# Attention scores from high and low parts, one buffer for the queries, query evacuations held back by a slot

## The chip, the cores and the metric

One core of a Trainium2 chip runs the whole program. The time is device microseconds of one execution. Three executions of the kernel before gave 1408.58, 1412.33 and 1412.37 us; the median is 1412.33. The engines are named as the profile names them: PE is TensorE, DVE VectorE, ACT ScalarE, POOL GpSimd, SP SyncE.

## What is computed

A block of a model: mLSTM mixer, cross attention to a memory, gated feed-forward, each with a norm ahead and a residual. The change touches the cross attention alone (sequence 1024, memory 256, 4 heads of 256, all float32):

```python
def cross_attn(xn, memn, w_q, w_kv, w_o):
    q = (xn @ w_q).reshape(Bsz, S, X_HEADS, X_DH)
    k, v = jnp.split(memn @ w_kv, 2, axis=-1)
    ...
    s = jnp.einsum('bshd,bmhd->bhsm', q, k).astype(F32) * (X_DH ** -0.5)
    p = jax.nn.softmax(s, axis=-1).astype(v.dtype)
    o = jnp.einsum('bhsm,bmhd->bshd', p, v).reshape(Bsz, S, D)
    return o @ w_o
```

## The kernel before

Every engine has its own program, written out by hand, and the programs meet only at semaphores. The order is set by strips of weights, 256 columns or rows wide. For the attention the list is mk 0 to 3 (keys), the last wo, mv 0 to 3 (values), q 0, then q 1, xo 0, q 2, xo 1, q 3, xo 2, and xo 3. A q strip makes the queries of one head in 4 groups (`r` 0 to 3; `r % 2` is the half of the head's 256 features, `r // 2` the half of the 1024 tokens), each of 24 matmuls of 512 columns into one bank of PSUM. An xo strip has 16 groups of 6 matmuls and adds one head's part of the output projection to the residual `xT`. Banks 0 to 3 of PSUM are taken in turn; `FREED` says which engine's count frees a bank, and `wait_bank` waits for it before the bank's next group.

Nearly every product on TensorE is made from two fp32r parts of each operand (`product`, lines 1861 to 1869): high by high, high by low, low by high. The high part is a copy on ScalarE into an fp32r tile, the low part is the rest, subtracted on VectorE. The scores are the exception: line 2069 multiplies `QH` (queries) by `KM` (keys) as plain fp32. A plain fp32 matmul has two records in the trace.

Work besides the groups hangs on `PARTS`, which gives each engine a list of parts ahead of group `r` of a strip. Head h's attention is `attn(h, p)`. Parts 0 to 3 stand ahead of groups 0 to 3 of strip q h+1, parts 4 and 5 ahead of groups 0 and 3 of strip xo h; for the last head parts 0 to 3 are at groups 4, 7, 9 and 12 of xo 2, and 4 and 5 at groups 1 and 4 of xo 3. For a tile of 256 tokens (p from 0 to 3) the work is: TensorE scores (L2069) into bank 4 or 5; VectorE maximum (L1472, L1473); ScalarE exponentials into `ptok`, which is `acc` (L977); in part p+1, VectorE reciprocal and normalising (L1464, L1466), TensorE four transposes (L2079), ScalarE high part `PAH` (L987), VectorE low part `PAL` (L1478). Parts 3 and 5 multiply by the values and split the result into `YH` and `YL` (L998, L1485), which the xo strip reads.

Query groups are copied out of PSUM by ScalarE (L1054), right behind each group, into two places used in turn: `VQ` for even heads and `SG` for odd ones. Keys lie in `KM`, values in `VM` (both in full fp32), and the values are split in strip q 0 by `vsplit` (L1003 and L1491). Beside all this the weights of the next strip are split: high on ScalarE behind the parts of slot 0 (L874), low on VectorE in slots 1 and 2 (L1574). VectorE adds the residual of each xo group (L1500). Each engine carries out its program in the order written.

Of the kernel before, what the change touches and what calls it, by code (L numbers as in the profile page):

```python
# [6 lines left out]
ALU = mybir.AluOpType  # L7
# [3 lines left out]
P = 128  # L11
# [5 lines left out]
def build_block(nc, x, mem, norm_mix, norm_x, norm_ffn, norm_mem, norm_final, a_w_in, a_conv_w, a_gate_b,  # L17
# [26 lines left out]
    for h in range(1, H):  # L44
# [5 lines left out]
    assert NF % 2 == 0  # L50
    NGROUPS = {"qk": 4, "v": 4, "o": 4, "wo": 16, "mk": 1, "mv": 1, "q": 4, "xo": 16,
               "gate": 4, "up": 4, "last": 24}
    BY_ACT = {"v", "o", "mk", "mv", "q", "gate"}
    FIRST, FREED, took = {}, [], {"act": 0, "dve": 0, "up": 0}
    GROUPS = [(n, r) for n, (kind, _) in enumerate(STRIPS) for r in range(NGROUPS[kind])]
    at = GROUPS.index((NF, 0))
# [10 lines left out]
    NB = 4  # L67
# [19 lines left out]
    def part(kind, h, r, what):  # L87
        PARTS.setdefault((AT[kind, h], r), []).append(what)
# [45 lines left out]
    for i in range(4):  # L134
        part("xo", H - 1, 12 + i, ("pieces", 4, (2 * i, 2 * i + 1)))
    for t in range(2):
        part("q", 0, 1 + t, ("vsplit", t, None))
    for h in range(1, H):
        for p in range(4):
            part("q", h, p, ("attn", h - 1, p))  # L140
# [23 lines left out]
    with ctx:  # L164
# [18 lines left out]
        def sem(name):  # L183
            return ctx.enter_context(nc.semaphore(name))
# [84 lines left out]
        ML = XL[:, 0:2, :].rearrange("p k s -> p (k s)").rearrange("p (k m) -> p k m", k=KT)  # L269
        KM = QK[:, 0].rearrange("p a s -> p (a s)").rearrange("p (k m) -> p k m", k=KT)  # L270
        VM = VQ[:, 0].rearrange("p (a d) -> p a d", a=MT)
        QH = [VQ[:, 1].rearrange("p (a s) -> p a s", a=2), SG[:, :, :]]
        ptok = acc[:, :, :]
        halves = lambda t: t.rearrange("p (a s) -> p a s", a=2)
        sqb = [None, halves(SG[:, 1, :]), acc[:, :, :]]
# [18 lines left out]
        S3L = sb_at("S3L", [P, 4, HALF], vv_at, F32R)  # L294
        PAH = sb_at("PAH", [P, MT, S], qk_at + 8192, F32R)
        PAL = sb_at("PAL", [P, MT, S], scan_at, F32R)
        VMH = sb_at("VMH", [P, MT, D], late_at, F32R)
        VML = sb_at("VML", [P, MT, D], vv_at, F32R)
        four = lambda t: t[:, :, :].rearrange("p a (b s) -> p (a b) s", b=2)
# [105 lines left out]
        s_mu = sem("s_mu")  # L405
        s_st = sem("s_st")
        s_wt = sem("s_wt")
        s_mask = sem("s_mask")
        s_wi = sem("s_wi")
        s_ks = sem("s_ks")  # L410
        s_pt = sem("s_pt")
# [16 lines left out]
        s_pt2 = sem("s_pt2")  # L428
        s_pa = sem("s_pa")
        s_pah = sem("s_pah")  # L430
        s_vmh = sem("s_vmh")
        s_vml = sem("s_vml")
        s_pv = sem("s_pv")
        s_sqn = sem("s_sqn")
        s_ssq = sem("s_ssq")
# [297 lines left out]
        def _(pool):  # L733
# [73 lines left out]
                        gp.tensor_tensor(lo, full, hi.bitcast(F32), ALU.subtract).then_inc(s_xlp, 1)  # L807

            todo = {"scan": scan, "memnorm": memnorm, "sumsq": sumsq, "pieces": pieces}
            for what in ("gates", "memturn", "spread", "attn", "vsplit"):  # L810
                todo[what] = lambda a, b: None

            sumsq(0, 0)
# [53 lines left out]
        def _(act):  # L867
# [132 lines left out]
            def vsplit(t, b):  # L1000

                act.wait_ge(s_fa, FREED[FIRST[AT["mv", H - 1]]][1])
                sc.activation(VMH[:, t, :], VM[:, t, :], ACT.Copy).then_inc(s_vmh, 1)  # L1003

            todo = {"gates": gates, "scan": scan, "memnorm": memnorm, "memturn": memturn,
                    "pieces": pieces, "attn": attn, "vsplit": vsplit}
            for what in ("sumsq", "spread"):
                todo[what] = lambda a, b: None

            def evac(n, r):  # L1010
                kind, h = STRIPS[n]
                g = FIRST[n] + r
                bank = PS[:, g % NB, :]
                if kind == "qk":

                    c = 4 * h + r
                    act.wait_ge(s_conv, c + 1)
                    if r == 0 and h >= 2:
                        act.wait_ge(s_b, TT * (h - 1))
                    at = (r // 2) * HALF  # L1020
                    sc.activation(QK[:, h % 2, r % 2, at:at + HALF], acc[:, r % 2, :], ACT.Tanh, scale=0.5).then_inc(s_ex1, 1)
                    return
                if kind not in BY_ACT:
                    return
                act.wait_ge(s_mm, g + 1)
                if kind == "v":
                    if r == 0 and h >= 2:
                        act.wait_ge(s_b, TT * (h - 1))
                    sc.activation(VV[:, h % 2, 2 * r:2 * r + 2, 0:DV], bank.rearrange("p (t d) -> p t d", t=2),
                                  ACT.Copy).then_inc(s_fa, 1)  # L1030
                elif kind == "o":
                    if r == 0 and h == 0:
                        act.wait_ge(s_gd, 5)
                    if r == 0 and h >= 1:
                        act.wait_ge(s_yf, TT * h)
                    sc.activation(SG[:, r % 2, (r // 2) * HALF:(r // 2 + 1) * HALF], bank,
                                  ACT.Tanh, scale=0.5).then_inc(s_fa, 1)
                elif kind == "mk":
                    if h == 0:
                        act.wait_ge(s_turn, TT + MT)  # L1040
                        act.wait_ge(s_xs, MT)
                    sc.activation(KM[:, 2 * h:2 * h + 2, :], bank.rearrange("p (t d) -> p t d", t=2),
                                  ACT.Copy).then_inc(s_fa, 1)
                elif kind == "mv":
                    sc.activation(VM[:, :, h * SW:(h + 1) * SW], bank.rearrange("p (t d) -> p t d", t=2),
                                  ACT.Copy).then_inc(s_fa, 1)
                elif kind == "q":
                    if r == 0 and h == 0:
                        act.wait_ge(s_b, TT * H)
                    if r == 0 and h == 1:  # L1050
                        act.wait_ge(s_xl, LO[3, LATE[1]][1])
                    if r == 0 and h >= 2:
                        act.wait_ge(s_sc, 4 * (h - 1))
                    sc.activation(QH[h % 2][:, r % 2, (r // 2) * HALF:(r // 2 + 1) * HALF], bank,  # L1054
                                  ACT.Copy).then_inc(s_fa, 1)

            def square_x(t):
# [22 lines left out]
            for n in range(NF):  # L1080
                kind, h = STRIPS[n]
                for r in range(NGROUPS[kind]):
                    run_parts(n, r, todo)
                    if r == 0:
                        split_hi(n + 1)
                        if held:
                            evac(*held.pop())
                    if NGROUPS[kind] == 1:
                        run_parts(n, "mid", todo)
                    if kind == "o" and h >= 1:  # L1090

                        if r == 3:
                            for q in range(4):
                                evac(n, q)
                    elif (kind, h) == ("wo", H - 1) or (kind, h) == ("xo", H - 1) and r < KT + 3:
                        square(n, r)
                    elif kind == "mv":
                        held.append((n, r))
                    else:
                        evac(n, r)  # L1100
                run_parts(n, "end", todo)
# [158 lines left out]
        def _(dve):  # L1260
# [67 lines left out]
            def scan(h, p):  # L1328
                if p < TT:
                    e = h * TT + p  # L1330
                    dve.wait_ge(s_wt, e + 1)
                    v.tensor_tensor(wT[:, e % 2, :], wT[:, e % 2, :], causal[:, :], ALU.min).then_inc(s_mask, 1)
                    dve.wait_ge(s_st, e + 1)
                    dve.wait_ge(s_mask, e + 1)
                    if e >= 2:
                        dve.wait_ge(s_b, e - 1)
                    v.scalar_tensor_tensor(out=wT[:, e % 2, :], in0=X1[:, 2 * P:3 * P], scalar=QSCALE, in1=wT[:, e % 2, :], op0=ALU.mult,
# [149 lines left out]

            def vsplit(t, b):

                dve.wait_ge(s_vmh, t + 1)  # L1490
                v.tensor_tensor(VML[:, t, :], VM[:, t, :], VMH[:, t, :].bitcast(F32), ALU.subtract).then_inc(s_vml, 1)  # L1491

            todo = {"gates": gates, "scan": scan, "memnorm": memnorm, "memturn": memturn, "vsplit": vsplit,
                    "sumsq": sumsq, "spread": lambda a, b: None, "pieces": pieces, "attn": attn}

            def add_residual(g, r):

# [4 lines left out]
            def evac(n, r):  # L1502
# [26 lines left out]
                elif kind == "v" and r == 0:  # L1529
                    finish_qk(h, 3)  # L1530
                elif kind == "o" and r == 3:
                    for q in range(4):
                        finish_o(n, q)
                elif kind not in BY_ACT:
                    add_residual(g, r)

# [25 lines left out]
            for n in range(NF):  # L1562
                kind, h = STRIPS[n]
                with_squares = kind in ("wo", "xo") and h == H - 1
                which = 1 if kind == "wo" else 2
                for r in range(NGROUPS[kind]):
                    run_parts(n, r, todo)
                    if kind == "mk":
                        run_parts(n, "mid", todo)
                    if NGROUPS[kind] == 1 or r in (1, 2):  # L1570
# [274 lines left out]
        def _(pe):  # L1845
# [209 lines left out]
            def attn(h, p):  # L2055
                if p < 4:
# [5 lines left out]
                    if p == 0 and h:  # L2062
                        pe.wait_ge(s_yl, H * TT + 4 * h)
                    if p == 0:
                        pe.wait_ge(s_fa, FREED[FIRST[AT["q", h]] + 3][1])
                    for j in range(2):
                        at = slice((2 * p + j) * P, (2 * p + j + 1) * P)
                        for kk in range(2):
                            last = mm(PS[:, NB + e % 2, j * M:(j + 1) * M], QH[h % 2][:, kk, at], KM[:, 2 * h + kk, :],  # L2069
                                      start=(kk == 0), stop=(kk == 1))  # L2070
                    last.then_inc(s_sc, 1)
                if 1 <= p <= 4:
                    e = 4 * h + p - 1
# [8 lines left out]
                if p in (3, 5):  # L2082
                    half = p // 2 - 1
                    pe.wait_ge(s_pa, 4 * h + 2 * half + 2)
                    for dt in range(2):
# [5 lines left out]
                        if p == 3 and dt == 1:  # L2091
                            pe.wait_ge(s_ex, 2 * (4 * h + 3))
                        if c == 0:
                            pe.wait_ge(s_vml, MT)
                        v_at = slice(h * DV + dt * P, h * DV + (dt + 1) * P)
                        p_at = slice(half * HALF, (half + 1) * HALF)
                        product((X3, X0)[dt], [((VMH[:, m, v_at], VML[:, m, v_at]), (PAH[:, m, p_at], PAL[:, m, p_at]))
                                               for m in range(MT)]).then_inc(s_pv, 1)

            todo = {"gates": gates, "scan": scan, "memnorm": lambda a, b: None, "memturn": memturn, "sumsq": sumsq,  # L2100
                    "spread": spread, "pieces": lambda a, b: None, "attn": attn, "vsplit": lambda a, b: None}

            def turn_x(t):

# [184 lines left out]
```

## Time and profile before

| | |
|---|---|
| median of 3 runs | 1412.33 us |
| profiled execution | 1410.57 us |
| its span, first to last instruction | 1408.8 us |
| mean granted clock of TensorE | 0.995 |
| PE busy | 1374.4 us, 98%, 6833 matmul records |
| PEld (weight loads) busy | 1162.9 us, 83% |
| DVE busy | 943.4 us, 67% |
| ACT busy | 492.4 us, 35% |
| POOL busy | 209.0 us, 15% |
| line 2069 in the chain that ended last | 1.9% of the span |

The query and output strips run from about 507 to 745 us. A row of a timeline gives the start in us, the duration in us, the engine, the line, the operation and its tiles (out<-in), shapes, a count, and in brackets the idle time of the engine before it and what ended that. Matmuls are pipelined: a 512-column one has a duration of 0.39 us and the next starts 0.23 us later, so the pace is read from starts. Equal tiles and shapes in a row are merged, as in "x8". The idle time of an engine that nobody waits for costs nothing.

### The profile page before, as it was taken

To read this page: it belongs to the slowest core of one execution; us is meant where nothing else is said; L and a number is where in the kernel's file an instruction comes from. 1 tells how busy PE (TensorE), PEld (TensorE's weight loads), DVE (VectorE), ACT (ScalarE), POOL (GpSimd) and SP (SyncE) were. 2 spreads that over 40 slices of the span, in tenths; PEclk is the share of its full clock that TensorE was granted. 3 is DMA by queue.
4 is the path that set the end of the run, shared out by engine and by line. 5 is a ranking of instruction groups with operands and counts; after the bars stand their busy time and mean duration, and the time that the engine had idled before them with its cause. 6 is when DMAs were issued, how large, how long until landed. Compare 5 with 4: busy or idle time off the path is not lost.

```text
span 1408.8 us, 18109 instructions
## 1 busy us (share of the span) xinstructions
PE 1374.4 (98%) x6833; PEld 1162.9 (83%) x6833; DVE 943.4 (67%) x1660; ACT 492.4 (35%) x868; POOL 209.0 (15%) x228
## 2 busy tenths in 40 slices
PE   7999999999998999999999999999999998999997
PEld 6988888889888878888877888888888887888887
DVE  5838458458377863554577976677787778877775
ACT  6323213313335453222334533343444434222222
POOL 5001201202303000000005000000000004444441
PEclk9999999999999999999999999999999999999999
DMA  5111201200313220010132132244444449799603
GB/s 181 41 50 31 60 31 31 60 30 31 105 61 107 74 88 32 30 60 7 54 120 105 46 113 98 75 165 159 140 142 164 145 168 366 263 305 316 237 30 120
DMA packets 109255, 156.44 MB, mean 111 GB/s; under 512 B 6448, under 2 KB 67952, under 8 KB 109168
## 3 DMA queue, kind: packets, MB, share of 16 engines
q1 hardware_dynamic: 109168, 155.28, 32.5%
q8 instruction: 55, 0.90, 0.3%
q14 instruction: 32, 0.26, 0.1%
HBM read 112.79 MB, written 42.47 MB: 110 GB/s over the span
## 4 chain that ended last, share of the span: by engine, by line
PE 64%; DVE 3%; issue 1%; ACT 0%; POOLq 0%; POOL 0%; ACTq 0%; DVEq 0%
PE PS L2185 9%; PE PS L2183 9%; PE PS L2184 9%; PE PS L1866 7%; PE PS L1867 6%; PE PS L1868 6%; PE PS L2213 4%; PE PS L2215 4%; PE PS L2214 4%; PE PS L2069 2%; DVE SG L1416 1%; PE PS L2079 0%; DVE xT L1500 0%; PE PS L2247 0%; DVE QK L1449 0%
## 5 line engine op out<-in xcount | busy, mean ns | idle before, releaser
L1866 PE MATMUL PS<-XH,WH 128*128 128x512 f32 (+1 forms) x448 | 174.8, 390 | 3.4 <-issue 3.3
L1868 PE MATMUL PS<-XH,WL 128*128 128x512 f32 (+1 forms) x448 | 168.5, 376 | 0.0
L1867 PE MATMUL PS<-XL,WH 128*128 128x512 f32 (+1 forms) x448 | 168.5, 376 | 0.0
L1500 DVE TENSOR_TENSOR xT<-PS,xT 128x512 f32<-128x512 f32 x128 | 87.6, 688 | 46.9 <-PE PS L1868 46.4
L1708 DVE TENSOR_TENSOR xT<-PS,xT 128x512 f32<-128x512 f32 x120 | 80.8, 688 | 43.2 <-PE PS L2215 42.9
L1866 PE MATMUL PS<-YH,WH 128*128 128x512 f32 x256 | 101.7, 397 | 0.7 <-issue 0.7
L1866 PEld LDWEIGHTS PS<-XH,WH 128*128 128x128 f32 x448 | 84.7, 189 | 19.5 <-issue 4.4
L1868 PE MATMUL PS<-YH,WL 128*128 128x512 f32 x256 | 99.8, 390 | 0.0
L1867 PE MATMUL PS<-YL,WH 128*128 128x512 f32 x256 | 99.7, 390 | 0.0
L1868 PEld LDWEIGHTS PS<-XH,WL 128*128 128x128 f32 x448 | 84.7, 189 | 15.8
L1867 PEld LDWEIGHTS PS<-XL,WH 128*128 128x128 f32 x448 | 84.7, 189 | 14.6
L1866 PE MATMUL PS<-WH,XH 128*128 128x256 f32 x320 | 92.6, 289 | 2.0 <-issue 2.0
L1868 PE MATMUL PS<-WH,XL 128*128 128x256 f32 x320 | 90.5, 283 | 0.0
L1867 PE MATMUL PS<-WL,XH 128*128 128x256 f32 x320 | 90.5, 283 | 0.0
L841 POOL TENSOR_TENSOR W2A<-raw,W2A 128x512 fp32r<-128x512 f32 x20 | 27.6, 1379 | 386.6 <-ACT W2A L1170 386.6
L1648 DVE TENSOR_TENSOR U<-PS,U 128x512 f32<-128x512 f32 x50 | 33.6, 688 | 55.7 <-PE PS L2185 55.7
L1574 DVE TENSOR_TENSOR WL<-raw,WH 128x1024 fp32r<-128x1024 f32 x54 | 65.8, 1227 | 5.0 <-ACT WH L874 5.0
L1866 PEld LDWEIGHTS PS<-WH,XH 128*128 128x128 f32 x320 | 61.2, 191 | 2.9 <-issue 2.4
L2183 PE MATMUL PS<-XH,WA 128*128 128x512 f32 x160 | 62.2, 389 | 0.0
L2185 PE MATMUL PS<-XH,WA 128*128 128x512 f32 x160 | 62.2, 389 | 0.0
L2183 PE MATMUL PS<-XH,WB 128*128 128x512 f32 x160 | 62.2, 389 | 0.0
L2185 PE MATMUL PS<-XH,WB 128*128 128x512 f32 x160 | 62.2, 389 | 0.0
(386 smaller groups left out, 3467.8 us busy)
## 6 DMA issues: line engine op xcount, KB each, us to landing
forms_hi<-HS SPq DMA_DIRECT2D x56, 256.0 KB, 2.4
raw<-in_f_w_up_dram SPq DMA_DIRECT2D x11, 1024.0 KB, 5.8
rawE<-in_f_w_gate_dram SPq DMA_DIRECT2D x10, 1024.0 KB, 5.7
raw<-in_f_w_down_dram SPq DMA_DIRECT2D x40, 256.0 KB, 3.8
raw<-in_a_w_in_dram SPq DMA_DIRECT2D x8, 1024.0 KB, 5.2
forms_lo<-U SPq DMA_DIRECT2D x32, 256.0 KB, 2.6
XH<-forms_hi SPq DMA_DIRECT2D x16, 512.0 KB, 6.4
XL<-forms_lo SPq DMA_DIRECT2D x12, 512.0 KB, 7.0
```

The lines of the kernel that those rows point to most:

```text
L1500: v.tensor_tensor(xt, PS[:, g % NB, :], xt, ALU.add).then_inc(s_fd, 1)
L1574: last = v.tensor_tensor(WL[:, (n + 1) % 2, at], raw_of(n + 1)[:, at], WH[:, (n + 1) % 2, at].bitcast(F32), ALU.subtract)
L1708: v.tensor_tensor(x, bank_of(g, which), x, ALU.add).then_inc(s_ee, 1)
L1866: mm(dst, wh, xh, start=(k == 0), stop=False)
L1867: mm(dst, wh, xl, start=False, stop=False)
L1868: last = mm(dst, wl, xh, start=False, stop=(k == len(tiles) - 1))
L2183: mm(bank, w[:, i, 0, at], xh[:, kk, :], start=start, stop=False, skip_group_check=True)
L2184: mm(bank, w[:, i, 0, at], xl[:, kk, :], start=False, stop=False, skip_group_check=True)
L2185: last = mm(bank, w[:, i, 1, at], xh[:, kk, :], start=False, stop=stop, skip_group_check=True)
L2213: mm(bank, w[:, i, 0, at], xh[:, u, :], start=start, stop=False, skip_group_check=True)
L2214: mm(bank, w[:, i, 0, at], xl[:, u, :], start=False, stop=False, skip_group_check=True)
L2215: last = mm(bank, w[:, i, 1, at], xh[:, u, :], start=False, stop=stop, skip_group_check=True)
```

## The change

The keys are split into `KMH` (heads 0 to 2 in one tile, head 3 in another) and `KML`, which lies where `KM` lies; this is the new part `ksplit`, two steps on ScalarE and VectorE in groups 1 and 2 of q 0, and `vsplit` moves one group later. The queries get one high tile `QHH` and one low tile `QHL` for all heads. ScalarE writes the high part, and VectorE subtracts it from the bank in `query_lo`; the bank is freed by VectorE now. Line 2069 becomes a `product` of high and low parts: twelve fp32r matmuls of 256 columns for a tile of 256 tokens where there were four plain ones. The evacuation of query group r is done in slot r+1, behind that slot's parts; that of group 3 at the head of the next strip, ahead of its parts, on ScalarE and on VectorE. A new wait on ScalarE keeps `QHH` until the scores of the head before have read it. In the scan of the mixer a wait for a semaphore of its own (`s_mask`) becomes the common chain of VectorE (`link`).

```diff
@@ ordering
-    BY_ACT = {"v", "o", "mk", "mv", "q", "gate"}
+    BY_ACT = {"v", "o", "mk", "mv", "gate"}
...
     for t in range(2):
-        part("q", 0, 1 + t, ("vsplit", t, None))
+        part("q", 0, 1 + t, ("ksplit", t, None))
+        part("q", 0, 2 + t, ("vsplit", t, None))
@@ tiles
-        QH = [VQ[:, 1].rearrange("p (a s) -> p a s", a=2), SG[:, :, :]]
+        KMH = [sb_at("KMH", [P, 6, M], late_at + 8192, F32R), sb_at("KMT", [P, 2, M], scan_at + 8192, F32R)]
+        KML = sb_at("KML", [P, 2 * H, M], qk_at, F32R)
+        QHH = sb_at("QHH", [P, 2, S], vv_at + 8192, F32R)
+        QHL = sb_at("QHL", [P, 2, S], place["SG"], F32R)
@@ ScalarE
+            def ksplit(t, b):
+
+                act.wait_ge(s_fa, FREED[FIRST[AT["mk", H - 1]]][1])
+                act.wait_ge(s_yl, H * TT)
+                sc.activation(KMH[t][:, :, :], KM[:, 6 * t:6 + 2 * t, :], ACT.Copy).then_inc(s_kvh, 1)
...
+                if kind == "q":
+                    act.wait_ge(s_mm, g + 1)
+                    if r == 0 and h == 0:
+                        act.wait_ge(s_b, TT * H)
+                    if r % 2 == 0 and h >= 1:
+                        act.wait_ge(s_sc, 4 * (h - 1) + 2 + r)
+                    sc.activation(QHH[:, r % 2, (r // 2) * HALF:(r // 2 + 1) * HALF], bank, ACT.Copy).then_inc(s_qh, 1)
                     return
...
                 for r in range(NGROUPS[kind]):
+                    if r == 0 and held and STRIPS[held[0][0]][0] == "q":
+                        evac(*held.pop())
                     run_parts(n, r, todo)
                     if r == 0:
                         split_hi(n + 1)
...
+                    elif kind == "q":
+                        if r:
+                            evac(*held.pop())
                         held.append((n, r))
@@ VectorE
-                    v.tensor_tensor(wT[:, e % 2, :], wT[:, e % 2, :], causal[:, :], ALU.min).then_inc(s_mask, 1)
+                    link(v.tensor_tensor(wT[:, e % 2, :], wT[:, e % 2, :], causal[:, :], ALU.min))
                     dve.wait_ge(s_st, e + 1)
-                    dve.wait_ge(s_mask, e + 1)
...
+            def ksplit(t, b):
+
+                dve.wait_ge(s_kvh, 2 * t + 1)
+                at = slice(6 * t, 6 + 2 * t)
+                v.tensor_tensor(KML[:, at, :], KM[:, at, :], KMH[t][:, :, :].bitcast(F32), ALU.subtract).then_inc(s_kvl, 1)
...
+            def query_lo(n, r):
+
+                hi, lo = (t[:, r % 2, (r // 2) * HALF:(r // 2 + 1) * HALF] for t in (QHH, QHL))
+                dve.wait_ge(s_qh, 4 * STRIPS[n][1] + r + 1)
+                v.tensor_tensor(lo, PS[:, GI[n, r] % NB, :], hi.bitcast(F32), ALU.subtract).then_inc(s_fd, 1)
...
+                elif kind == "q":
+                    split_late.append((n, r))
...
                 for r in range(NGROUPS[kind]):
+                    if r == 0 and split_late:
+                        query_lo(*split_late.pop())
                     run_parts(n, r, todo)
+                    if split_late:
+                        query_lo(*split_late.pop())
@@ TensorE, attn
                     if p == 0:
-                        pe.wait_ge(s_fa, FREED[FIRST[AT["q", h]] + 3][1])
+                        pe.wait_ge(s_fd, FREED[FIRST[AT["q", h]] + 3][1])
+                        pe.wait_ge(s_kvl, 3)
                     for j in range(2):
                         at = slice((2 * p + j) * P, (2 * p + j + 1) * P)
-                        for kk in range(2):
-                            last = mm(PS[:, NB + e % 2, j * M:(j + 1) * M], QH[h % 2][:, kk, at], KM[:, 2 * h + kk, :],
-                                      start=(kk == 0), stop=(kk == 1))
+                        keys = lambda k: (KMH[k // 6][:, k % 6, :], KML[:, k, :])
+                        last = product(PS[:, NB + e % 2, j * M:(j + 1) * M],
+                                       [((QHH[:, kk, at], QHL[:, kk, at]), keys(2 * h + kk)) for kk in range(2)])
```

## Rows read from the trace of the kernel before

**Rows 1.** The page, busy time of each engine over the span.

```profile
PE 1374.4 (98%) x6833; PEld 1162.9 (83%) x6833; DVE 943.4 (67%) x1660; ACT 492.4 (35%) x868; POOL 209.0 (15%) x228
```

**Rows 2.** Busy us by stretch: PE, PEld, DVE, ACT, POOL, clock, DMA.

```profile
530.00:562.00 32.00, 31.77 (x147) 26.68 (x148) 11.93 (x27) 10.33 (x26) 0.00 (x0) 1.00 0.10 34
562.00:588.00 26.00, 26.00 (x118) 21.50 (x117) 14.62 (x20) 4.09 (x5) 0.00 (x0) 1.00 0.13 41
```

**Rows 3.** Timeline of PE, scores in two slots and their neighbours.

```profile
537.52 1.89 PE L2069 MATMUL PS<-QK,VQ 128*128 128x256 f32 x8
539.25 0.60 PE L2079 MATMUL PS<-ident,acc 128*128 128x128 f32 x4
...
587.45 0.39 PE L1866 MATMUL PS<-YH,WH 128*128 128x512 f32 x1
...
588.13 1.89 PE L2069 MATMUL PS<-QK,SG 128*128 128x256 f32 x8
...
590.55 0.39 PE L1866 MATMUL PS<-XH,WH 128*128 128x512 f32 x1
```

**Rows 4.** Timeline of PE: fp32r products of 256 columns; entry to 512 columns.

```profile
485.08 0.28 PE L1866 MATMUL PS<-WH,XH 128*128 128x256 f32 x1
485.20 0.28 PE L1867 MATMUL PS<-WL,XH 128*128 128x256 f32 x1
...
75.38 0.47 PE L1866 MATMUL PS<-XH,WH 128*128 128x512 f32 x1
75.69 0.40 PE L1867 MATMUL PS<-XL,WH 128*128 128x512 f32 x1
```

**Rows 5.** Timelines of ACT and PE at the start of q 1.

```profile
529.49 0.60 ACT L1054 ACTIVATE VQ<-PS 128x512 f32<-128x512 f32 x1 [4.84 <-PE PS L1868]
530.23 1.97 PE L2069 MATMUL PS<-QK,VQ 128*128 128x256 f32 x8 [0.78 <-ACT VQ L1054]
```

**Rows 6.** Timelines of DVE, PE and ACT around the start of xo 0.

```profile
559.35 0.62 DVE L1466 TENSOR_SCALAR acc<-acc,small 128x256 f32<-128x256 f32 x2
...
563.16 0.60 PE L2079 MATMUL PS<-ident,acc 128*128 128x128 f32 x4
...
563.36 0.60 ACT L1054 ACTIVATE SG<-PS 128x512 f32<-128x512 f32 x1 [4.85 <-PE PS L1868]
563.86 0.59 ACT L987 ACTIVATE PAH<-PS 128x512 fp32r<-128x512 f32 x1
...
564.48 0.69 DVE L1478 TENSOR_TENSOR PAL<-PS,PAH 128x512 fp32r<-128x512 f32 x1 [4.52 <-ACT PAH L987]
```

**Rows 7.** Timelines of DVE and PE at group 1 of xo 3.

```profile
717.18 0.69 DVE L1500 TENSOR_TENSOR xT<-PS,xT 128x512 f32<-128x512 f32 x1 [0.67 <-PE PS L1868]
...
718.64 0.66 PE L2079 MATMUL PS<-ident,acc 128*128 128x128 f32 x4 [1.50 <-DVE acc L1466]
```

**Rows 8.** Timeline of DVE in q 1; then line 1491 (duration ns min/median/max).

```profile
543.85 0.62 DVE L1466 TENSOR_SCALAR acc<-acc,small 128x256 f32<-128x256 f32 x2
...
L1491 DVE TENSOR_TENSOR VML<-VQ,VMH x2: 1218/1222/1227, 519.7 to 521.9; 128x1024 fp32r<-128x1024 f32 x2
```

**Rows 9.** Timeline of PE behind two gaps; stretches as in rows 2, with clock.

```profile
507.12 0.47 PE L1866 MATMUL PS<-XH,WH 128*128 128x512 f32 x1 [2.06 <-issue]
...
757.04 1.05 PE L2036 MATMUL PS<-ones,SG 128*128 128x1 f32 x8 [1.90 <-DVE SG L1416]
...
759.02 0.63 PE L1867 MATMUL PS<-XL,WH 128*128 128x512 f32 x1
759.45 0.63 PE L1868 MATMUL PS<-XH,WL 128*128 128x512 f32 x1
...
506.00:508.00 2.00, 0.88 (x4) 0.78 (x5) 2.00 (x3) 0.29 (x1) 0.00 (x0) 1.00 0.00 0
...
759.00:760.00 1.00, 1.00 (x4) 0.79 (x3) 0.00 (x0) 0.00 (x0) 0.68 (x1) 0.50 1.08 350
...
762.00:763.00 1.00, 1.00 (x5) 0.85 (x4) 0.00 (x0) 0.00 (x0) 0.00 (x0) 0.85 0.00 0
```

More of the change, by code:

```diff
@@ L407, in build_block @@
         s_wt = sem("s_wt")
-        s_mask = sem("s_mask")
         s_wi = sem("s_wi")
@@ L430, in build_block @@
         s_pah = sem("s_pah")
-        s_vmh = sem("s_vmh")
-        s_vml = sem("s_vml")
+        s_kvh = sem("s_kvh")
+        s_kvl = sem("s_kvl")
+        s_qh = sem("s_qh")
         s_pv = sem("s_pv")
@@ L809, in _ @@
             todo = {"scan": scan, "memnorm": memnorm, "sumsq": sumsq, "pieces": pieces}
-            for what in ("gates", "memturn", "spread", "attn", "vsplit"):
+            for what in ("gates", "memturn", "spread", "attn", "vsplit", "ksplit"):
                 todo[what] = lambda a, b: None
@@ L1002, in vsplit @@
                 act.wait_ge(s_fa, FREED[FIRST[AT["mv", H - 1]]][1])
-                sc.activation(VMH[:, t, :], VM[:, t, :], ACT.Copy).then_inc(s_vmh, 1)
+                sc.activation(VMH[:, t, :], VM[:, t, :], ACT.Copy).then_inc(s_kvh, 1)
+            def ksplit(t, b):
+                act.wait_ge(s_fa, FREED[FIRST[AT["mk", H - 1]]][1])
+                act.wait_ge(s_yl, H * TT)
+                sc.activation(KMH[t][:, :, :], KM[:, 6 * t:6 + 2 * t, :], ACT.Copy).then_inc(s_kvh, 1)
             todo = {"gates": gates, "scan": scan, "memnorm": memnorm, "memturn": memturn,
-                    "pieces": pieces, "attn": attn, "vsplit": vsplit}
+                    "pieces": pieces, "attn": attn, "vsplit": vsplit, "ksplit": ksplit}
             for what in ("sumsq", "spread"):
@@ L1021, in evac @@
                     sc.activation(QK[:, h % 2, r % 2, at:at + HALF], acc[:, r % 2, :], ACT.Tanh, scale=0.5).then_inc(s_ex1, 1)
+                    return
+                if kind == "q":
[5 more added lines that the diff above has]
+                    sc.activation(QHH[:, r % 2, (r // 2) * HALF:(r // 2 + 1) * HALF], bank, ACT.Copy).then_inc(s_qh, 1)
                     return
@@ L1046, in evac @@
                                   ACT.Copy).then_inc(s_fa, 1)
[L1047 to L1055, printed above, removed]
             def square_x(t):
@@ L1097, in _ @@
                     elif kind == "mv":
+                        held.append((n, r))
+                    elif kind == "q":
+                        if r:
+                            evac(*held.pop())
                         held.append((n, r))
@@ L1488, in vsplit @@
             def vsplit(t, b):
-                dve.wait_ge(s_vmh, t + 1)
-                v.tensor_tensor(VML[:, t, :], VM[:, t, :], VMH[:, t, :].bitcast(F32), ALU.subtract).then_inc(s_vml, 1)
-            todo = {"gates": gates, "scan": scan, "memnorm": memnorm, "memturn": memturn, "vsplit": vsplit,
-                    "sumsq": sumsq, "spread": lambda a, b: None, "pieces": pieces, "attn": attn}
+                dve.wait_ge(s_kvh, 2 * t + 2)
+                v.tensor_tensor(VML[:, t, :], VM[:, t, :], VMH[:, t, :].bitcast(F32), ALU.subtract).then_inc(s_kvl, 1)
+            def ksplit(t, b):
+                dve.wait_ge(s_kvh, 2 * t + 1)
+                at = slice(6 * t, 6 + 2 * t)
+                v.tensor_tensor(KML[:, at, :], KM[:, at, :], KMH[t][:, :, :].bitcast(F32), ALU.subtract).then_inc(s_kvl, 1)
+            todo = {"gates": gates, "scan": scan, "memnorm": memnorm, "memturn": memturn, "vsplit": vsplit, "ksplit": ksplit,
+                    "sumsq": sumsq, "spread": lambda a, b: None, "pieces": pieces, "attn": attn}
+            split_late = []
+            def query_lo(n, r):
+                hi, lo = (t[:, r % 2, (r // 2) * HALF:(r // 2 + 1) * HALF] for t in (QHH, QHL))
+                dve.wait_ge(s_qh, 4 * STRIPS[n][1] + r + 1)
+                v.tensor_tensor(lo, PS[:, GI[n, r] % NB, :], hi.bitcast(F32), ALU.subtract).then_inc(s_fd, 1)
             def add_residual(g, r):
@@ L2093, in attn @@
                         if c == 0:
-                            pe.wait_ge(s_vml, MT)
+                            pe.wait_ge(s_kvl, 2 * MT)
                         v_at = slice(h * DV + dt * P, h * DV + (dt + 1) * P)
@@ L2100, in _ @@
             todo = {"gates": gates, "scan": scan, "memnorm": lambda a, b: None, "memturn": memturn, "sumsq": sumsq,
-                    "spread": spread, "pieces": lambda a, b: None, "attn": attn, "vsplit": lambda a, b: None}
+                    "spread": spread, "pieces": lambda a, b: None, "attn": attn, "vsplit": lambda a, b: None, "ksplit": lambda a, b: None}
             def turn_x(t):
```

## Prediction

> **What bounds the kernel now.** I read the page's engine line first: TensorE is busy for 98% of the span [rows 1]. An average over stages does not say who is waited for in the attention, so the second view is the table of stretches. In the query strips and the output strips between them TensorE has no gap: 31.77 of 32 us, then 26.00 of 26, at a granted clock of 1.00, while VectorE works 11.93 and 14.62 us there and ScalarE 10.33 and 4.09 [rows 2]; the two stretches stand for five (530 to 678 us), which repeat them. So a microsecond taken from TensorE there is gained whole, and a microsecond for which TensorE waits is lost whole. Spare time of VectorE is cover only for work that TensorE doesn't wait for. The third view is the timeline of the places where the change puts something between TensorE and the operand that it needs next.
>
> I call the time in which TensorE makes one group of a strip a slot. "q1 slot 3" is the fourth group of ("q", 1).
>
> **The change part by part.**
>
> *Scores.* Sixteen times, four plain fp32 products of 256 columns (two records each) become twelve fp32r products. In a slot in which transposes follow, the scores run from 537.52 to 539.25, 1.73 us [rows 3]. The replacement has the form of the memory keys' products, 128x256 with a load of weights each, which start 0.12 us apart [rows 4]: 12 x 0.12 = 1.44 us, a gain of 0.29 in 12 places. In the 4 places where a group follows at once, the scores take from 588.13 to the second L1866 at 590.55, less the usual step 588.13 - 587.45 = 0.68, so 1.74 us [rows 3]; afterwards 1.44 and an entry to the next group like 75.38 to 75.69 (0.31 where 0.23 is the pace, and 0.03 before it) [rows 4], about 1.55: a gain of 0.19. Sum 12 x 0.29 + 4 x 0.19 = 4.2 us, all on TensorE's path. Bounds: 3.0 (0.19 everywhere) and 4.6 (0.29 everywhere).
>
> The Trainium skill (FP8 and Floating Point Precision, section on TensorE precision) gives true fp32 four passes, and TensorE: Matmul & The Clock Gate (Back-to-back issue gap) N/2.4 + 2.5 ns each; an estimate from these would be 64 x 109 ns = 7.0 us, and + 0.4 in place of + 3.2 in the sum below. The memory keys' rows are slower than that, 0.12 against 0.109, and they decide. The same page (Part 3, The mechanism) says that a weight load overlaps a running matmul only on another row group; with the loads in series the gain would be gone, and the sum 4.2 us higher. The pace of 0.12 us with one load each [rows 4] speaks against it here.
>
> *Splitting keys.* ScalarE gets two copies (1536 and 512 columns) and VectorE two subtractions in q0. The nearest VectorE row is the split of the values, 1.22 us for 1024 columns [rows 8], so about 1.8 and 0.65 us. VectorE starts at about 519.6 as before and then has 2.45 (keys) + 2.45 (values) + 2.4 (weights of q1) + three low parts at 0.65: done near 529, and the high part of q0's last group comes only at 530.1. Hidden, with 1 us to spare. The weights of q1 are ready near 527, the load for xo0 starts 2.5 us later than before, and both are wanted after 531.
>
> *Start of q1.* Before, TensorE waited for ScalarE's copy of q0's last group (start 529.49, scores at 530.23) [rows 5]. Now VectorE's low part stands behind it: 529.49 + 0.62 (from a ScalarE copy to the VectorE operation behind it, 563.86 to 564.48 [rows 6]) + 0.69 + 0.04 = 530.84. Cost 0.6 us; bounds 0.5 and 1.0.
>
> *Held evacuations inside the query strips.* The evacuation of group r is now behind the attention part of slot r+1 on both engines, and its bank is wanted four groups later. VectorE's extra 0.65 us per slot lies between the low part of the probabilities and the next normalising, which ends near 544.5 [rows 8] where the transposes that need it start about 546.9 (one slot of 7.6 us behind 539.25 [rows 3]): 2.4 us of slack, less 0.65 and less what the shorter scores take (0.3), leaves 1.4. Cost nothing; if the cover were gone, each us of overshoot would count in about eight slots. The new wait on the scores of the head before (one place for queries) is already met, since TensorE makes those scores at the head of the slot. The mask wait of the scan goes to an equivalent wait of VectorE on itself: nothing. SyncE and GpSimd get no instruction.
>
> *The last group of q1, q2 and q3.* This is the step that decides. In the first slot of xo0, xo1 and xo2 TensorE starts with four transposes of the normalised probabilities. Before, VectorE normalised them long ahead (559.35), and TensorE went through at 563.16 with no gap; ScalarE copied the last query group beside it (563.36) [rows 6]. After, VectorE has `query_lo` of that last group at the head of this slot, ahead of reciprocal and normalising. VectorE takes its work in order, so the normalising waits for the end of the matmuls, ScalarE's copy and the subtraction, and TensorE for all of it. The same kind of wait stands already in xo3: from the start of a 0.69 us operation through reciprocal and normalising to the transposes, 717.18 to 718.64, 1.46 us, with TensorE idle 1.50 [rows 7]. With the copy ahead: 563.36 + 0.62 + 1.46 = 565.44 instead of 563.16, so 2.28 us. Three times: 6.8 us. Bounds: 4.9 (3 x 1.64, as if the copy were free) and 7.5 (a quarter us of entry each). Everything behind moves along with TensorE, so nothing downstream gives it back.
>
> *The clock.* Rows of this trace show both ends for such a gap. After an idle 2.06 us the clock stayed at 1.00 (2.4 GHz); after an idle 1.90 and eight one-column products it fell to 0.50 (1.2 GHz) at 759.0 and came back near 762.3 [rows 9]. The new gap, 2.28 us and 0.36 of transposes, lies between these two (2.1 and 2.8 us without a dense matmul). So I take even odds for each, one or two of three. Price: matmuls start 0.43 apart instead of 0.23 for 3.3 us [rows 9], eight of them, 1.6 us for each fall; bounds none and 4.8 for all three.
>
> **Sum** on the profiled execution's own time, 1410.6 us (span 1408.8 and 1.8 around it): - 4.2 + 0.6 + 6.8 = + 3.2 before the clock; with one fall + 4.8, with two + 6.4. The middle is + 5.6, 1416.2 us. The median of the runs shown is 1.8 above the profiled execution, and they spread over 3.8; a change within 0.3%, 4.2 us, is about what a measurement of this kernel can't tell from none.
>
> **Rivals.**
> (a) The clock is held in all three gaps: + 3.2, 1413.8 us, which is no measurable change. For it: the 2.06 us gap that cost nothing [rows 9]. This ends on the other side; the point from which it decides is whether a gap of this length lets the clock fall.
> (b) All three gaps let it fall: + 8.0, 1418.6. For it: the fall at 759.0.
> (c) The gap in the xo strips doesn't come, because the normalising is finished before the low part: - 4.2 + 0.6 = - 3.6, 1407.0. The change would then do what a reader of TensorE's column alone expects. Against it: the order of VectorE's program, and the 1.50 us of xo3 [rows 7].
> (d) VectorE falls behind in q0 or inside the slots: up to 2 us more at q1 and in slots with a weight split, 1418 or so. Against it: 11.93 of 32 us busy [rows 2].
>
> **How the numbers follow.** The forecast (one or two falls) 0.50; (a) 0.29; (b) 0.11; (c) 0.05; (d) 0.05. Its own range is 1414 to 1418.5. One fall (+4.8) is just over the bound, so of the forecast's half I give 0.42 to slower, 0.07 to no change and 0.01 to faster (a pace of the products under 0.12); of (a), with the size of the stall uncertain, 0.06 and 0.23; (b) and (d) are slower but for 0.01; (c) is split, 0.03 to no change and 0.02 to faster. Slower 0.63, same 0.34, faster 0.03. The range takes in (a) less the bounds of its terms (1.9 on the stalls, 0.4 on the scores), (b), and the distance of the runs' median: 1411.5 to 1420.5.
>
> **What would show each step.** The scores' twelve products in 1.44 us, where 1.73 stood. TensorE idle about 2.3 us, three times, before L2079's transposes, released by VectorE's normalising, with `query_lo` right before the reciprocal. About 1.4 us idle before the first scores. In the table of stretches, 3 to 4 us of granted clock near 0.5 behind one or two of these gaps. No idle time inside the query strips. I am wrong if the transposes at the head of xo0 start without a gap, if the products start over 0.14 us apart, or if VectorE's normalising inside a query strip ends after the transposes could start.

## The result, and the profile after

The changed kernel takes 1416.67 us (median of 8 runs, 1414.65 to 1419.93) against 1410.88 us (8 runs, 1408.58 to 1412.56) before: + 5.8 us, ratio 1.0038 with a 95% interval of 1.0027 to 1.0049, which is + 3.8 to + 6.9 us. The forecast was + 5.6. The profiled execution of after took 1415.1 us (span 1413.4).

The page's engine line answers to [rows 1]. TensorE is busy 2.2 us less, in a span that is 4.5 us longer; columns as there.

```profile
PE 1372.2 (97%) x6897; PEld 1163.4 (82%) x6897; DVE 955.9 (68%) x1678; ACT 493.8 (35%) x870; POOL 208.8 (15%) x228
```

The timeline of PE in after, for the scores with transposes behind them (540.25) and with a group behind them (592.29), answers to [rows 3]:

```profile
538.81 0.28 PE L1900 MATMUL PS<-KMH,QHH 128*128 128x256 f32 x1
538.93 0.28 PE L1901 MATMUL PS<-KML,QHH 128*128 128x256 f32 x1
...
540.25 0.60 PE L2114 MATMUL PS<-ident,acc 128*128 128x128 f32 x4
...
590.85 0.28 PE L1900 MATMUL PS<-KMH,QHH 128*128 128x256 f32 x1
...
592.29 0.40 PE L1900 MATMUL PS<-XH,WH 128*128 128x512 f32 x1
592.98 0.40 PE L1900 MATMUL PS<-XH,WH 128*128 128x512 f32 x1
```

Twelve products take 538.81 to 540.25, 1.44 us, where 1.73 stood; the next group is entered at its normal step (592.29 to 592.98, 0.69). Now the start of q 1, ACT, DVE and PE in after, which answers to [rows 5]:

```profile
530.43 0.60 ACT L1039 ACTIVATE QHH<-PS 128x512 fp32r<-128x512 f32 x1 [4.84 <-PE PS L1902]
531.06 0.69 DVE L1522 TENSOR_TENSOR QHL<-PS,QHH 128x512 fp32r<-128x512 f32 x1 [3.13 <-ACT QHH L1039]
531.85 0.36 PE L1900 MATMUL PS<-KMH,QHH 128*128 128x256 f32 x1 [1.46 <-issue]
```

TensorE is idle for 1.46 us instead of 0.78. The profile puts it down to "issue", but the three rows stand in a row: copy, subtraction, first product 0.10 us behind it. VectorE had been idle for 3.13 us, so the split of the keys was out of the way. The rows that decide are those at the head of xo 0, in the same order; they answer to [rows 6]:

```profile
563.33 0.39 PE L1902 MATMUL PS<-XH,WL 128*128 128x512 f32 x1
...
563.75 0.60 ACT L1039 ACTIVATE QHH<-PS 128x512 fp32r<-128x512 f32 x1 [4.35 <-PE PS L1902]
...
564.38 0.69 DVE L1522 TENSOR_TENSOR QHL<-PS,QHH 128x512 fp32r<-128x512 f32 x1 [4.15 <-ACT QHH L1039]
564.99 0.15 DVE L1478 RECIPROCAL small<-small 128x2 f32<-128x2 f32 x1
565.18 0.62 DVE L1480 TENSOR_SCALAR acc<-acc,small 128x256 f32<-128x256 f32 x2
...
565.85 0.66 PE L2114 MATMUL PS<-ident,acc 128*128 128x128 f32 x4 [2.13 <-DVE acc L1480]
```

The last matmul of q 1 starts at 563.33, so with the pace of 0.23 the transposes were due at 563.56; they start at 565.85, 2.29 us late. VectorE, idle for 4.15 us ahead of this, could have normalised long before, but the low part of the last query group stood in front of it. xo 1 and xo 2 show the same:

```profile
624.82 0.66 PE L2114 MATMUL PS<-ident,acc 128*128 128x128 f32 x4 [2.14 <-DVE acc L1480]
683.79 0.66 PE L2114 MATMUL PS<-ident,acc 128*128 128x128 f32 x4 [2.14 <-DVE acc L1480]
```

The clock, stretches as in [rows 9], in after:

```profile
563.00:566.00 3.00, 0.86 (x5) 0.40 (x4) 1.38 (x4) 0.60 (x1) 0.00 (x0) 1.00 0.00 0
566.00:568.00 2.00, 2.00 (x12) 1.70 (x12) 0.76 (x2) 1.46 (x2) 0.00 (x0) 1.00 0.00 0
...
684.00:686.00 2.00, 2.00 (x9) 1.60 (x8) 0.69 (x1) 1.51 (x2) 0.00 (x0) 0.60 0.00 0
686.00:688.00 2.00, 2.00 (x7) 1.57 (x6) 1.01 (x2) 0.89 (x1) 0.00 (x0) 0.55 0.00 0
```

Behind the gap of xo 0 the clock stayed at 1.00; behind that of xo 2, of the same length, it fell to 0.50 for 3.4 us (684.4 to 687.8). One fall of three in this execution.

**The books of the stage.** From q 0's last matmul to xo 3's last one it is 529.07 to 743.87 before, 214.8 us, and 530.00 to 750.05 after, 220.1: + 5.3 us. Three gaps of 2.29 are 6.9, the start of q 1 0.7, one fall of the clock 1.6; together 9.2, so the shorter scores are left with 3.9. Line by line they give 16 x 0.29 = 4.6; the rest goes into entries behind the gaps (0.41 us from the transposes to the next group at 565.85, where it is 0.35 at 540.25) and small waits in xo 2. The 1.6 for a fall can be read from rows: from the transposes at the head of xo 2 to the next scores it is 10.76 us in after (683.79 to 694.55), and 9.17 in gap_short below (678.02 to 687.19), where the clock held, so 1.59.

### The profile page after: what moved, and what is told of

It reads as the page before. It is cut to its first block, busy times and chain, and to the rows that moved or that the text cites. A ratio compares the mean times of both kernels' runs of the same rounds, so it can differ in the third digit from the quotient of the medians.

```text
span 1413.4 us, 18265 instructions
## 1 busy us (share of the span) xinstructions
PE 1372.2 (97%) x6897; PEld 1163.4 (82%) x6897; DVE 955.9 (68%) x1678; ACT 493.8 (35%) x870; POOL 208.8 (15%) x228
## 4 chain that ended last, share of the span: by engine, by line
PE 88%; DVE 7%; issue 2%; DMA 1%; ACT 1%; SPq 1%; POOL 0%; POOLq 0%; DVEq 0%; ACTq 0%
PE PS L1900 14%; PE PS L1901 14%; PE PS L1902 14%; PE PS L2218 8%; PE PS L2220 8%; PE PS L2219 8%; PE PS L2248 4%; PE PS L2250 4%; PE PS L2249 4%; PE PS L2042 1%; PE PS L2046 1%; PE PS L2044 1%; DVE SG L1430 1%; PE PS L1963 1%; DVE xT L1528 1%
```

## Experiments

Times are medians, each with the ratio to the kernel before on the same chip; "before" is 1411.47 us (16 runs) for the first four kernels and 1409.80 us (15 runs) for the others. These are two chips: the kernel before is 1.7 us apart on them, and 0.2 when both are brought to one clock (how, stands under norm_first_early). A difference between kernels of the two groups is therefore given at one clock as well. The theory **order** says: VectorE's program order costs 2.29 us at each of three places. Its rivals are **load** (VectorE has too much to do, wherever it stands), **products** (the new products or their weight loads cost more than they show), and for the clock **count** (a gap costs only its own length), against **clock** (a gap can also let the clock fall) and **phase** (where the gap lies in time has a say in that).

**after_again** is the changed kernel once more.

> The changed kernel as it is, as the reference for its neighbours on this chip. Every theory: 5 to 6 us over the kernel before. Theory order (VectorE's low part of the last query group stands ahead of the normalising): three gaps of TensorE of 2.1 to 2.2 us idle at the heads of xo 0, 1 and 2. Theory phase (the clock falls behind a gap or not by where the gap lies in time, not by its length alone): the gaps are as long as in the first profile, but the clock may fall behind other ones of them.

Measured 1416.81 us (1.0040, 1.0027 to 1.0054). The gaps are 2.14 us idle again. The mean clock is 0.992 in the profile, and this time there are falls behind xo 2's gap, as in the first profile, and behind an older one at 760 us, where the first one had none. So at 760 us the same gap of the same program had a fall in one execution and none in the other; at the three new gaps the pattern stayed.

**norm_first** moves one operation of VectorE, three times.

```diff
-                    if r == 0 and split_late:
+                    if r == 0 and split_late and kind == "q":
                         query_lo(*split_late.pop())
                     run_parts(n, r, todo)
```

> One line: at the head of the xo strips VectorE does the attention part (reciprocal, normalising) first and query_lo after it; at the head of q 1 the order stays. Theory order: the three gaps vanish (3 x 2.29 = 6.9 us) and with them the clock falls behind them (0 to 4.8): 7 to 9 us below after_again, 1.5 to 3 us below the kernel before, since the shorter scores (16 x 0.3) less the longer wait at q 1 (0.7) are left. Rival load (VectorE is too full with the new splits, wherever they stand): the gaps stay or move into the slots, under 3 us gained. Rival products (the new products and their weight loads cost what the profile hides): still above the kernel before.

Measured 1407.75 us (0.9974, 0.9964 to 0.9984): 9.1 us below after_again and 3.7 below the kernel before. VectorE and PE of norm_first at the same place:

```profile
558.17 0.68 DVE L1522 TENSOR_TENSOR QHL<-PS,QHH 128x512 fp32r<-128x512 f32 x1
558.76 0.15 DVE L1478 RECIPROCAL small<-small 128x2 f32<-128x2 f32 x1
558.96 0.62 DVE L1480 TENSOR_SCALAR acc<-acc,small 128x256 f32<-128x256 f32 x2
...
562.17 0.60 PE L2114 MATMUL PS<-ident,acc 128*128 128x128 f32 x4
...
564.10 0.68 DVE L1522 TENSOR_TENSOR QHL<-PS,QHH 128x512 fp32r<-128x512 f32 x1
```

The normalising is done 2.6 us ahead of the transposes, which have no idle time, and the low part of the last group (564.10) stands behind the attention part. The work is the same, so load falls, and with it products: without the gaps the kernel is faster than the one before.

**norm_first_early** also lets TensorE start a head's scores once the groups of their tokens are there.

```diff
                     if p == 0:
-                        pe.wait_ge(s_fd, FREED[FIRST[AT["q", h]] + 3][1])
+                        pe.wait_ge(s_fd, FREED[FIRST[AT["q", h]] + 1][1])
                         pe.wait_ge(s_kvl, 3)
+                    if p == 2:
+                        pe.wait_ge(s_fd, FREED[FIRST[AT["q", h]] + 3][1])
```

> norm_first, and TensorE waits ahead of the first scores of a head only for the query groups 0 and 1, which hold the tokens of the first two tiles, and for groups 2 and 3 ahead of the third tile. Theory order: the idle time ahead of q 1's scores (1.46 us) goes, so 1.5 us below norm_first and about 4 us below the kernel before. Rival: the wait only moves, because groups 0 and 1 have their low parts late in q 0 (VectorE is busy with keys and values there); then under 0.5 us below norm_first.

Measured 1407.41 us (0.9967, 0.9954 to 0.9980). The idle time at q 1 is gone from the profile, as expected: in the waits of PE (us in total, times, longest) "issue" stands at 7.5 in 6 times in norm_first and here at

```profile
PE PS L1900 <- issue: 6.0, 5, 2.1
```

The medians differ by only 0.3 us, though, which is what the rival (the wait only moves) expected. The medians of this pair alone don't show the 1.5 us: the mean clock of the runs was 0.9930 here and 0.9948 in norm_first. Over all 91 runs of these kernels the time goes up by 0.93 us for each 0.001 of mean clock (one slope fitted within the kernels), and brought to one clock (0.994) the means of the pair are 1408.3 and 1406.6 us, 1.7 apart. The profiles say the same without a fit: from q 0's last matmul to xo 3's last one it is 211.3 us in norm_first and 209.6 here, with the clock at 1.00 throughout in both, so the wait did not move.

**before_stalled** puts the suspected wait alone into the kernel before.

```diff
                 for r in range(NGROUPS[kind]):
+                    if kind == "xo" and r == 0 and h < H - 1:
+                        dve.wait_ge(s_fa, FREED[FIRST[AT["q", h + 1]] + 3][1])
+                        v.tensor_tensor(T[:, 0].rearrange("p a b -> p (a b)"), xT[:, 0, 0:HALF], xT[:, 1, 0:HALF], ALU.add)
                     run_parts(n, r, todo)
```

> The kernel before with the suspected wait alone: at the head of xo 0, 1 and 2 VectorE first waits for ScalarE's copy of the last query group and does one 512-column addition into an unused tile, then the attention part. Scores, queries and all else stay. Theory order: three gaps of 2.1 to 2.2 us idle, 6.9 us, and 0 to 4.8 us of clock: 7 to 10 us above the kernel before. Rival load or products: the gap needs the new splits, so under 3 us.

Measured 1420.31 us (1.0059, 1.0043 to 1.0076), 8.8 us above the kernel before. The gap is that of after, without any of its new work, and here the clock fell behind two of the three. PE at xo 0, and the stretch behind it:

```profile
566.29 1.11 PE L2082 MATMUL PS<-ident,acc 128*128 128x128 f32 x4 [2.14 <-DVE acc L1466]
```

```profile
566.00:568.00 2.00, 1.71 (x6) 1.58 (x7) 0.23 (x1) 0.56 (x2) 0.00 (x0) 0.53 0.00 0
```

**gap_short** is norm_first with shorter gaps.

```diff
+                    if r == 0 and split_late:
+                        dve.wait_ge(s_mm, GI[split_late[0]] + 1)
                     run_parts(n, r, todo)
```

> norm_first (no gap at the xo strips), but VectorE waits there for the end of the last query group before it normalises. The copy and the subtraction don't stand in between, so each gap is 2.29 less 0.62 and 0.61, about 1.05 us. Both theories: 3.1 us above norm_first. Theory clock: no stretch at 0.50 behind these three gaps, and the mean clock stays that of norm_first (0.995); theory count says nothing of the clock.

Measured 1411.21 us (1.0007, 0.9997 to 1.0018), 3.5 us above norm_first and 3.1 at one clock, the expected 3.1. The gap at xo 0, and no clock below 1.00 behind any of the three:

```profile
562.53 0.66 PE L2116 MATMUL PS<-ident,acc 128*128 128x128 f32 x4 [0.91 <-DVE acc L1480]
```

**gap_long** is the changed kernel with longer gaps.

```diff
                     if r == 0 and split_late:
-                        query_lo(*split_late.pop())
+                        query_lo(*split_late.pop(), times=3 if kind == "xo" else 1)
...
+                for i in range(times - 1):
+                    link(v.tensor_tensor(lo, PS[:, GI[n, r] % NB, :], hi.bitcast(F32), ALU.subtract))
```

> The changed kernel, with query_lo done three times over at the heads of xo 0, 1 and 2, which makes each of the three gaps 1.4 us longer (2.1 to 3.5 us idle). Theory count (a gap costs its own length and nothing else): 4.2 us above the changed kernel, mean clock as there (0.992). Theory clock (a gap also lets the clock fall, the likelier the longer it is, 1.6 us each time): every one of the three gaps is followed by a stretch at 0.50, the mean clock is lower (about 0.990), and the time 5.5 to 8 us above the changed kernel.

Measured 1422.60 us (1.0088, 1.0071 to 1.0104), 5.9 us above after and 4.9 at one clock; the gaps grew by 4.4. Its five runs have a mean clock of 0.9908 against 0.9925 and 0.9920, a difference no larger than single runs of one kernel show, so the medians alone don't refute count. The traces do: the clock fell behind two of these gaps, the first time for 6.8 us (627.9 to 634.8), and a fall in dense matmuls costs time, 1.59 us by the rows above. But the expectation that every gap would be followed by a fall missed: behind the first one the clock stayed. PE at that gap, then the stretches behind the three:

```profile
568.32 0.65 PE L2116 MATMUL PS<-ident,acc 128*128 128x128 f32 x4 [3.59 <-DVE acc L1480]
```

```profile
568.00:572.00 4.00, 3.68 (x18) 3.13 (x19) 2.20 (x5) 2.40 (x2) 0.00 (x0) 1.00 0.00 0
628.00:632.00 4.00, 3.26 (x10) 2.78 (x11) 1.34 (x4) 2.11 (x2) 0.00 (x0) 0.50 0.00 0
694.00:696.00 2.00, 2.00 (x6) 1.61 (x5) 0.98 (x3) 1.10 (x1) 0.00 (x0) 0.50 0.00 0
```

**no_hold** is norm_first with the query groups 0 to 2 evacuated right behind themselves.

```diff
+                    elif kind == "q" and r < 3:
+                        evac(n, r)
                     elif kind == "q":
-                        if r:
-                            evac(*held.pop())
                         held.append((n, r))
...
+                elif kind == "q" and r < 3:
+                    query_lo(n, r)
                 elif kind == "q":
                     split_late.append((n, r))
```

> norm_first without the held evacuation of query groups 0 to 2: both engines do them right behind the group, ahead of the next slot's attention part. One place for queries makes ScalarE wait for scores that TensorE makes only in the next slot, for groups 0 and 2; the normalising that the next transposes need stands behind all this. Theory order: TensorE waits 2.3 us in slots 1 and 3 and 0.85 us in slot 2 of q 1, 2 and 3, 16 us above norm_first, and more with the clock. Rival (the holding back is of no use, since ScalarE has time to spare in these strips): within 2 us of norm_first.

Measured 1430.30 us (1.0135, 1.0112 to 1.0157), 22.6 us above norm_first; at one clock 18.4. The rival, that the holding back is of no use, is refuted. The gaps came where and as long as expected, 5.1 us in each query strip; PE of no_hold in q 1:

```profile
541.06 0.66 PE L2116 MATMUL PS<-ident,acc 128*128 128x128 f32 x4 [2.19 <-DVE acc L1480]
549.33 0.66 PE L2116 MATMUL PS<-ident,acc 128*128 128x128 f32 x4 [0.71 <-DVE acc L1480]
559.08 0.66 PE L2116 MATMUL PS<-ident,acc 128*128 128x128 f32 x4 [2.20 <-DVE acc L1480]
```

So with one buffer for the queries it is the holding back that makes their low parts affordable inside the strips. In slots 1 and 3 ScalarE's copy waits for scores as well, since there is one place for the queries; in slot 2 it doesn't, and the order alone costs 0.71 us. A kernel with two places and no holding back wasn't run. The stage is 230.2 us long in this profile, 18.8 more than in norm_first: 15.3 of idle time, 1.6 for one fall (622.1 us), and some 0.2 at each of the nine gaps, by which the transposes and the group behind them come later than the idle time says (537.27 to 541.47 is 4.20 us where norm_first has 1.79, so 2.41 for a gap of 2.19).

**best** takes norm_first_early and removes the like gap that both kernels had in xo 3, by normalising the last tile ahead of the residual of xo 3's first group.

```diff
+            def attn(h, p):
+                if 1 <= p <= 4 and (h, p) != (H - 1, 4):
+                    normalise(h, p)
...
                     run_parts(n, r, todo)
+                    if (kind, h, r) == ("xo", H - 1, 0):
+                        normalise(H - 1, 4)
```

> norm_first_early, and the last tile's normalising stands ahead of the residual of xo 3's first group instead of behind it. Theory order: the idle time of 1.5 us in xo 3 goes too, 1.5 us below norm_first_early, some 5.5 us below the kernel before. Rival (what TensorE gains there is waited for again in xo 3, where the residual and the squares on VectorE set the end of the stage): within 0.5 us of norm_first_early.

Measured 1404.52 us (0.9958, 0.9943 to 0.9972), 2.9 us below norm_first_early and 2.3 at one clock, against 1.5 expected. The stage is 1.3 us shorter in the profile (208.3 for 209.6, no fall in either); what the medians show above that is within the spread of five runs. The wait that stood in [rows 7] with 1.50 us is 0.2 in all:

```profile
PE PS L2120 <- DVE acc L1478: 0.2, 1, 0.2
```

It beats both kernels: 5.3 us under the one before on the same chip, and about 11 under the changed one at one clock (12 by the medians).

**All profiles side by side.** The stage runs from q 0's last matmul to xo 3's last one. Idle is what gaps of TensorE over 0.6 us add up to in it, less the same in the kernel named. Falls are stretches of 3.4 us at 0.50 inside it, in this kernel and in the one named (the 6.8 us of gap_long count as two):

| kernel | stage, us | against | longer by | idle | falls |
|---|---|---|---|---|---|
| before | 214.8 | | | | |
| before_stalled | 225.0 | before | 10.2 | 6.4 | 2, 0 |
| norm_first | 211.3 | before | - 3.5 | 0.7 | 0, 0 |
| after | 220.1 | norm_first | 8.7 | 6.4 | 1, 0 |
| gap_short | 214.7 | norm_first | 3.4 | 2.7 | 0, 0 |
| gap_long | 227.2 | after | 7.2 | 4.4 | 3, 1 |
| no_hold | 230.2 | norm_first | 18.8 | 15.3 | 1, 0 |

With 1.6 us for each fall and 0.2 for each new gap the rows come out within 0.4 us (norm_first against before apart, where the scores are what differs).

## Why the prediction was right, step by step

**The bound.** TensorE without a gap, so each us on it counts: held. before_stalled added 6.9 us of gaps there and nothing else on TensorE, and lost 7.7 us at one clock.

**Scores.** Forecast 4.2, bounds 3.0 to 4.6; measured 4.6 by the rows and 3.9 net. The pace (0.12) and the 1.44 us were right. The term for the 4 places without transposes was sized too small, since the entry to the next group costs nothing; small waits in xo 2 took as much back (from its first scores to the transposes of xo 3 it is 30.98 us in before and 30.24 in norm_first, 0.74 gained where 4 x 0.29 were due). The estimate from the Trainium skill (FP8 and Floating Point Precision, TensorE Precision Notes; TensorE: Matmul & The Clock Gate, Back-to-back issue gap), 7.0 us, was too high. Its four passes agree with the trace: four plain products take 1.73 us, 0.108 us for each of 16 passes. Its pace for the new products, 0.109 us, doesn't: they start 0.12 us apart. The Trainium skill's other rule (TensorE: Matmul & The Clock Gate, The mechanism), that a load overlaps a matmul only on another row group, isn't borne out here: 12 products with 12 loads take 1.44 us. The same section also has loads pulled ahead into a background weight buffer, and that the trace doesn't contradict.

**Splitting keys, held evacuations, scan.** Nothing on the path, as forecast: in the stretch from 532 to 562 us of after TensorE is busy for 30.00 of 30 us, and VectorE was idle for 3.13 us at the end of q 0, where the forecast had 1 us to spare. The slack inside q 1 is 1.5 us (normalising done at 546.06, transposes at 547.59), forecast 1.4. That the hold costs nothing was stated as slack; no_hold showed that it is worth at least 15 us, which I had not worked out.

**Start of q 1.** Forecast + 0.6; measured 1.46 idle for 0.78, + 0.7.

**The last query group.** Forecast 2.28 us, three times; measured 2.29 in the profile (the two bounds should have read 5.0 and 7.6, for 4.9 and 7.5), and 9.1 us for all three together with the clock by norm_first. This is the step that turned a gain of 4 into a loss.

**The clock.** Forecast one or two falls behind three gaps; seen 1, 1 and 2 in the three profiles with gaps of that length. The means fit: the runs of after had a mean clock of 0.9925 and 0.9920, those of the kernel before 0.9944, which at 0.93 us for each 0.001 is 2.0 us, against 2.4 forecast. The odds were taken from the length of the gap. That was only half right: equal gaps differed, a gap of 3.59 us had no fall behind it, and the older gap of 2.06 us at 507 us, which had none in [rows 9], had one in after (0.50 from 507 to 510 us). What decides beside the length I have not settled; that the moment of the gap matters is an inference from this. The chances don't follow from the odds either: even odds for each of three gaps give none and three the same chance, and the prediction gave 0.29 and 0.11. And that the middle of the forecast and the median agree to 0.2 us is luck: the interval of the measurement alone is 3 us wide, and one fall more or less is 1.6.

**Rivals.** (a) and (b), no fall and three falls, can't be ruled out for a single execution; none of the three profiles showed either for gaps of 2.1 us, and the other runs have no trace. (c) is refuted by the rows at 564.38, (d) by the 3.13 us at the end of q 0 and, inside the slots, by the 30.00 of 30 us.

## What to carry to other kernels

When an operation moves onto an in-order engine, look at what stands behind it in that engine's program, not at how busy the engine is: here a 0.69 us subtraction on an engine with 4 us of idle time cost TensorE 2.29 us, because it waited for the newest result and stood ahead of work that was ready long before. Put what the bounding engine needs next first, and what frees a buffer four groups later last. And a gap in a TensorE that was full costs more than its length now and then: the nine us won by norm_first are some seven of gap and two of clock.

## What the runs showed of the hardware

Runs of one kernel spread by 1.6 us (best, 5 runs) to 7.0 us (norm_first, 11 runs), and much of that goes with how often the clock fell: the same program, the changed kernel, had mean clocks from 0.990 to 0.995. Two versions that differ by 1.5 us (norm_first and norm_first_early) can't be told apart by the medians of 5 to 11 runs; the length of the stage in the profile, or times brought to one clock, tell them apart.

How often the clock fell behind a gap of TensorE, over the ten profiles: behind the 2.14 us gaps of after, after_again and before_stalled in 4 of 9 cases; behind the like gaps of no_hold (2.2 us) in 1 of 6; behind the older gap of 2.05 us at 507 us in 5 of 10; behind the older one of 1.9 us ahead of the one-column products in 6 of 10; behind the 3.59 us gaps in 2 of 3. Behind the shorter ones, 0.7 to 1.5 us, between 530 us and the end of xo 3 it never fell, and in that stretch no fall stood away from a gap: each began between 0.8 us before the end of a gap and 1.3 us behind it. A gap of about 2 us is thus a chance of a fall, and the prediction's two rows (one held, one fell) were a small sample of it.
